# RWKV preparation moved into the loop of the mixing projection in a bidirectional encoder layer on one core

## The reference, cut to what matters

```python
proj = h @ w_in
gla_p, rw_p = proj[..., :GLA_COLS], proj[..., GLA_COLS:]
...
prev = jnp.pad(rw_p[:, :-1], ((0, 0), (1, 0), (0, 0)))
nxt = jnp.pad(rw_p[:, 1:], ((0, 0), (0, 1), (0, 0)))
rw = rw_p + rwkv_mu_prev * (prev - rw_p) + rwkv_mu_next * (nxt - rw_p)
r, kr, vr, wd_f, wd_b, ad, gd = _split(rw, RWKV_SPLITS)
...
dec_f = decay(wd_f, rwkv_w0_fwd, rwkv_w_up_fwd)
dec_b = decay(wd_b, rwkv_w0_bwd, rwkv_w_up_bwd)
a = jax.nn.sigmoid((rwkv_a0 + ad @ rwkv_a_up).astype(f32))
gate = (jax.nn.sigmoid(gd) @ rwkv_g_up).astype(f32)
kk = heads(kr * rwkv_k_k, RWKV_HEAD)
kk = kk / jnp.maximum(jnp.sqrt(jnp.sum(jnp.square(kk), axis=-1, keepdims=True)), 1e-12)
k2 = heads(kr * (1.0 + (a - 1.0) * rwkv_k_a), RWKV_HEAD)
```

## Time and profile before

| what | us |
|---|---|
| median of 3 runs | 4152.99 (4149.44 to 4160.55) |
| the profiled execution's own time | 4160.51 |
| its span, from first to last instruction | 4158.5 |
| mixing projection, first matmul to the store of the last tile | 1033.9 to 1417.2 |
| GLA | 1421.6 to 1656.6 |
| preparation, first load issued to first load of the recurrence | 1657.55 to 1839.88 |

### The profile page before, as it was taken

How to read it: one execution, slowest core, us unless ns; L and a number is a source line. 1 busy time by engine, 2 the same in 40 slices (tenths; PEclk the granted TensorE clock), 3 DMA queues, 4 the chain that set the end, 5 groups by cost and what they waited for, 6 DMA issues and landing times. The chain is left out here.

```text
span 4158.5 us, 68522 instructions
## 1 busy us (share of the span) xinstructions
PE 3614.8 (87%) x28536; PEld 3070.8 (74%) x28536; DVE 1872.7 (45%) x2671; ACT 927.5 (22%) x1295; POOL 225.8 (5%) x348
## 2 busy tenths in 40 slices
PE   7999999996999737449989688887897999999997
PEld 6888888885888536238888566776786888888885
DVE  4445444546000275765555532421225444444446
ACT  2111111103111245532323332222213111111112
POOL 0000000000000043012222100000000000000000
PEclk9999999998999868779999889998998999999999
DMA  2101010101222201652222122001001010101001
GB/s 107 46 30 45 30 45 30 45 5 42 109 79 87 114 1 42 195 183 91 75 74 75 73 98 109 15 31 41 31 26 41 31 45 30 45 30 45 30 20 51
DMA packets 70891, 243.80 MB, mean 59 GB/s; under 512 B 5056, under 2 KB 30912, under 8 KB 64448
## 3 DMA queue, kind: packets, MB, share of 16 engines
q1 hardware_dynamic: 64528, 219.39, 15.0%
q10 hardware_dynamic: 6192, 21.89, 1.3%
HBM read 185.22 MB, written 56.05 MB: 58 GB/s over the span
## 5 line engine op out<-in xcount | busy, mean ns | idle before, releaser
L292 DVE TENSOR_TENSOR main_acc<-main_acc,ffn_psum 128x512 f32<-128x512 f32 (+1 forms) x1056 | 617.7, 598 | 853.6 <-PE ffn_psum L215 853.0
L204 PE MATMUL ffn_psum<-x_xh,ffn_wi_h 128*128 128x512 f32 (+1 forms) x2112 | 525.1, 357 | 49.0 <-DVE ffn_wi_l L281 49.0
L204 PE MATMUL ffn_psum<-x_xh,ffn_wi_l 128*128 128x512 f32 (+1 forms) x2112 | 525.1, 357 | 0.0
L204 PE MATMUL ffn_psum<-x_xl,ffn_wi_h 128*128 128x512 f32 (+1 forms) x2112 | 525.0, 357 | 0.0
L204 PEld LDWEIGHTS ffn_psum<-x_xh,ffn_wi_h 128*128 128x128 f32 x2112 | 372.6, 188 | 116.9 <-DVE ffn_wi_l L281 49.4
L204 PEld LDWEIGHTS ffn_psum<-x_xh,ffn_wi_l 128*128 128x128 f32 x2112 | 349.8, 188 | 60.6
L204 PEld LDWEIGHTS ffn_psum<-x_xl,ffn_wi_h 128*128 128x128 f32 x2112 | 349.3, 188 | 61.1
L215 PE MATMUL ffn_psum<-ffn_hid_h,ffn_wo_h 128*128 128x512 f32 (+1 forms) x1056 | 380.5, 360 | 12.7 <-DVE ffn_hid_l L300 10.0
L215 PE MATMUL ffn_psum<-ffn_hid_h,ffn_wo_l 128*128 128x512 f32 (+1 forms) x1056 | 377.5, 358 | 0.0
L215 PE MATMUL ffn_psum<-ffn_hid_l,ffn_wo_h 128*128 128x512 f32 (+1 forms) x1056 | 376.6, 357 | 0.0
L256 ACT CAST ffn_hid_h<-ffn_hid 128x1280 fp32r<-128x1280 f32 x44 | 55.6, 1264 | 1090.4 <-DVE ffn_hid L298 1090.4
(11 more groups left out here) (303 smaller groups left out, 5629.2 us busy)
## 6 DMA issues: line engine op xcount, KB each, us to landing
ffn_w_raw_in<-ffn_w_in_dram SPq DMA_DIRECT2D x44, 1024.0 KB, 7.2
rws_pack<-pack SPq DMA_DIRECT2D x40, 900.0 KB, 6.3
ffn_w_raw_out<-ffn_w_out_dram SPq DMA_DIRECT2D x44, 512.0 KB, 3.5
proj<-mixin_stage ACTq DMA_DIRECT2D x27, 640.0 KB, 3.0
mixin_w_raw<-mix_w_in_dram SPq DMA_DIRECT2D x27, 512.0 KB, 3.4
pack<-rwp_pack SPq DMA_DIRECT2D x4, 2580.0 KB, 10.6
rwp_raw<-proj SPq DMA_DIRECT2D x15, 640.0 KB, 8.8
kv_w_raw<-ca_w_kv_dram SPq DMA_DIRECT2D x16, 512.0 KB, 3.5
```

The costliest lines, as they stand in the source:

```text
L204: mm = nc.tensor.matmul(ps[:, at + c * BANK:at + c * BANK + tn], w[:, slot, cols], x[:, k, t0:t0 + tn], start=(k == 0 and j == 0), stop=(k ...
L292: nc.vector.tensor_tensor(acc[:, o, t0:t0 + tn], acc[:, o, t0:t0 + tn], ps[:, at:at + tn], ALU.add).then_inc(added, 1)
```

## The change

The 27 tiles come in another order (by a new order of the weight columns): three low-rank tiles first, then for each group kr, r, vr, then the twelve GLA tiles. `linear_phase` for the mixing projection becomes `mixin_phase`, written out without a loop. The RWKV tiles are no longer stored to DRAM: ACT scales them straight out of PSUM and DVE adds the shifted copies from PSUM, each as one operation on 20 chunks of 63 columns and two on the chunk edges. The preparation's f32 matmuls (four products and two head sums per group, three chunks each) stand between k steps, one after a k step, into two further PSUM banks that are freed chunk by chunk; sigmoids, gate copies, clamps and bonus work on chunks. A PSUM set of an RWKV tile is free when its shifts are done (`next_added`). ACT and DVE run the steps of the preparation in a fixed order between the weight splits. The six work tiles lie in `main_acc`, once the residual has gone to DRAM (`spilled`). SP's queue holds weights, pack, gate and bonus stores in one order. The tile that holds the GLA gates' low-rank inputs is also stored raw. `rwkv_prepare_phase` and its loads are gone. `free_piece` waits until the piece two before (the same bank) was read; `high_part`, `low_part` and `project` are the old L386, L418 and one k step; `stayed` is L1075 with PSUM as its input, behind a wait for the tile's product; `logs` holds the old L1133 to L1146.

```diff
-Q_TILE, K_TILE, V_TILE, G_TILE = 0, 2, 4, 8
-R_TILE, KR_TILE, VR_TILE = 12, 16, 20
-DECAY_TILE, LOW_TILE, GATE_TILE = 24, 25, 26
-MIX_TILES = 27
+Q_TILE, K_TILE, V_TILE, G_TILE, LOW_TILE = 0, 2, 4, 8, 12
+GLA_TILES = 13
+N_LOW, N_RKV = 3, 12
+N_GLA = N_LOW + N_RKV
+MIX_TILES = N_GLA + 12
...
+        decay, aa, gate, run, kr, sums = [acc[:, 0], acc[:, 1]], acc[:, 2], acc[:, 3], acc[:, 4], acc[:, 5], acc[:, 6]
...
+            at = (6 + piece(kind, t, c) % 2) * BANK
+            return ps[:, at:at + TOKEN_CHUNKS[c][1]]
...
         @block.sync
         def _(sp):
...
+            weight(2)
+            weight(3)
...
+            sp.dma_start(resid_d, acc).then_inc(spilled, 16)
+            weight(4)
+            weight(5)
+            sp.wait_ge(low_copied, 1)
+            sp.dma_start(proj_d[LOW_TILE], low[:, 2]).then_inc(low_stored, 16)
+            weight(6)
             for t in range(4):
+                weight(tile(KR, t) + 4)
+                weight(tile(R, t) + 4)
                 sp.wait_ge(b_packed, t + 1)
                 sp.dma_start(pack_d[:, :, t, K_COL:PACK].rearrange("c p w -> p c w"), pack[:, :, K_COL:PACK]).then_inc(stored_b, 16)
+                sp.wait_ge(gate_done, NC * (t + 1))
+                sp.dma_start(gate_d[:, t], gate).then_inc(gate_stored, 16)
...
+                weight(tile(VR, t) + 4)
+                sp.wait_ge(centred, 4 * (t + 1))
+                sp.wait_ge(next_added, 3 * (tile(VR, t) + 1))
+                sp.dma_start(pack_d[:, :, t, 0:K_COL].rearrange("c p w -> p c w"), pack[:, :, 0:K_COL]).then_inc(stored_a, 16)
+                sp.wait_ge(bonus_done, NC * (t + 1))
+                sp.dma_start(bonus_d[:, t], sums).then_inc(bonus_stored, 16)
...
         @block.tensor
         def _(pe):
...
+            def logits(kind, t, c):
+                j, src, ready = {F_SIG: (0, 0, 1), B_SIG: (1, 0, 1), AA: (2, 1, 0), GATE: (3, 2, 2)}[kind]
...
+                free_piece(kind, t, c)
+                nc.tensor.matmul(piece_ps(kind, t, c), lora[:, t % 2, j * P:(j + 1) * P], low[:, src, tokens(c)],
+                                 start=True, stop=True).then_inc(pieced, 1)
+
+            def head_sums(kind, t, c):
+                pe.wait_ge(ones_in, 16)
+                pe.wait_ge((squared, rk_done)[kind == RK], t + 1)
+                free_piece(kind, t, c)
+                nc.tensor.matmul(piece_ps(kind, t, c), head_ones[:], sums[:, tokens(c)], start=True, stop=True).then_inc(pieced, 1)
...
+            def begin(n):
+                pe.wait_ge(split, n + 1)
+                if N_GLA <= n - 2:
+                    pe.wait_ge(emptied, n - 2 - N_GLA + 1)
+                elif n >= 2:
+                    pe.wait_ge(next_added, 3 * (n - 1))
...
             for t in range(4):
+                begin(tile(KR, t))
+                for k in range(KT):
+                    project(tile(KR, t), k)
+                    if t and 2 <= k < 5:
+                        head_sums(RK, t - 1, k - 2)
+                    if k >= 5:
+                        logits(AA, t, k - 5)
+                begin(tile(R, t))
+                for k in range(KT):
+                    project(tile(R, t), k)
+                    if k < 3:
+                        logits(F_SIG, t, k)
+                    if k >= 5:
+                        head_sums(KK, t, k - 5)
+                begin(tile(VR, t))
+                for k in range(KT):
+                    project(tile(VR, t), k)
+                    if k < 3:
+                        logits(B_SIG, t, k)
+                    if k >= 5:
+                        logits(GATE, t, k - 5)
+            for n in range(N_GLA, MIX_TILES):
...
         @block.scalar
         def _(act):
...
             for t in range(4):
                 if t:
+                    act.wait_ge(b_packed, t)
+                for c in range(NC):
+                    sigmoid(AA, t, aa, A0 + t, c)
...
+                stayed(tile(KR, t), view(kr), 4 + t)
+                high_part(tile(KR, t) + 2)
...
+                for c in range(NC):
+                    sigmoid(F_SIG, t, decay[0], W0 + t, c)
+                act.wait_ge(kk_raw, t + 1)
+                if t:
+                    act.wait_ge(bonus_stored, 16 * t)
+                nc.scalar.activation(view(sums), part(KK_COL), ACT.Square).then_inc(squared, 1)
+                if t:
+                    act.wait_ge(stored_a, 16 * t)
+                stayed(tile(R, t), part(R_COL), t)
+                high_part(tile(R, t) + 2)
+                for c in range(NC):
+                    sigmoid(B_SIG, t, decay[1], W0 + 4 + t, c)
+                act.wait_ge(clamped, NC * (t + 1))
...
+                stayed(tile(VR, t), part(V_COL), 8 + t)
+                high_part(tile(VR, t) + 2)
...
         @block.vector
         def _(dve):
...
+                nc.vector.scalar_tensor_tensor(dst[:, :, 1:], src[:, :, :-1], mu_p, dst[:, :, 1:], ALU.mult, ALU.add).then_inc(prev_added, 1)
+                for c0, cn in SEQ_CHUNKS:
+                    nc.vector.scalar_tensor_tensor(dst[:, c0 + 1:c0 + cn, 0:1], src[:, c0:c0 + cn - 1, C - 1:C], mu_p,
+                                                   dst[:, c0 + 1:c0 + cn, 0:1], ALU.mult, ALU.add).then_inc(prev_added, 1)
...
             for t in range(4):
+                shift(tile(KR, t), view(kr), 4 + t)
+                if t:
+                    dve.wait_ge(stored_b, 16 * t)
+                dve.wait_ge(next_added, 3 * (tile(KR, t) + 1))
+                nc.vector.tensor_scalar(part(KK_COL), view(kr), vecs[:, K_K + t:K_K + t + 1], None, ALU.mult).then_inc(kk_raw, 1)
+                low_part(tile(KR, t) + 2)
...
+                logs(t, 0)
+                for c in range(NC):
+                    dve.wait_ge(pieced, piece(KK, t, c) + 1)
...
+                shift(tile(R, t), part(R_COL), t)
+                low_part(tile(R, t) + 2)
...
+                logs(t, 1)
...
+                shift(tile(VR, t), part(V_COL), 8 + t)
+                low_part(tile(VR, t) + 2)
...
-        rwkv_prepare_phase(nc, a, proj_d, pack_d, vecs, side_d[0], side_d[1], consts)
...
-    proj_d = nc.dram_tensor("proj", (MIX_TILES, P, T), F32, kind="Internal").ap()
+    proj_d = nc.dram_tensor("proj", (GLA_TILES, P, T), F32, kind="Internal").ap()
...
-            linear_phase(nc, "mixin", weights, MIX_TILES, xh, xl, TOKEN_CHUNKS, "store", proj_d, spill=(acc[:], resid_d))
+            mixin_phase(nc, weights, a, xh, xl, acc[:], resid_d, proj_d, pack_d, vecs, side_d[0], side_d[1])
...
+    rkv = [u[:, t * P:(t + 1) * P] for t in range(4) for u in (kr, r, vr)]
+    out["mix_w_in"] = output_tiles(np.concatenate([wdf, wdb, ad, gdf, gdb, pad, gd] + rkv + [q, k, v, gg], 1))
```

More of the change, by code:

```diff
@@ L1060, in _ @@
+            for n in range(N_GLA, MIX_TILES):
+                begin(n)
+                for k in range(KT):
+                    project(n, k)
+                    if n == N_GLA and 2 <= k < 5:
+                        head_sums(RK, 3, k - 2)
         @block.scalar
         def _(act):
[L1062 to L1065 removed]
@@ new lines, in sigmoid @@
+            def sigmoid(kind, t, dst, bias, c):
+                act.wait_ge(pieced, piece(kind, t, c) + 1)
+                nc.scalar.activation(dst[:, tokens(c)], piece_ps(kind, t, c), ACT.Sigmoid, bias=vecs[:, bias:bias + 1]).then_inc(sig_done, 1)
+            high_part(0)
+            high_part(1)
+            stayed(0, view(low[:, 0]), 12)
+            high_part(2)
+            act.wait_ge(product, 2)
+            nc.scalar.copy(low[:, 2], slot(1)).then_inc(low_copied, 1)
+            act.wait_ge(low_copied, 1)
@@ L1097, in _ @@
-                nc.scalar.activation(raw[:, 1], raw[:, 1], ACT.Exp, scale=-0.5).then_inc(rooted, 1)
+                for c in range(NC):
+                    act.wait_ge(pieced, piece(GATE, t, c) + 1)
+                    nc.scalar.copy(gate[:, tokens(c)], piece_ps(GATE, t, c)).then_inc(gate_done, 1)
+                stayed(tile(VR, t), part(V_COL), 8 + t)
+                high_part(tile(VR, t) + 2)
+            for n in range(N_GLA, MIX_TILES):
+                i = n - N_GLA
+                act.wait_ge(product, n + 1)
+                if i >= 2:
+                    act.wait_ge(stored[n % 2], 16 * (i // 2))
+                nc.scalar.copy(stage(n), slot(n)).then_inc(emptied, 1)
+                act.wait_ge(emptied, i + 1)
+                act.dma_start(proj_d[i], stage(n)).then_inc(stored[n % 2], 16)
+                high_part(n + 2)
@@ L1099, in _ @@
+            for s in stored:
+                act.wait_ge(s, 16 * 6)
         @block.vector
@@ L1157, in _ @@
-                dve.wait_ge(kk_summed, t + 1)
-                nc.vector.tensor_scalar(raw[:, 1], sets[0], KK_EPS * KK_EPS, None, ALU.max).then_inc(clamped, 1)
+                nc.vector.tensor_tensor(part(K_COL), part(K_COL), view(kr), ALU.mult).then_inc(k_packed, 1)
+                logs(t, 0)
+                for c in range(NC):
+                    dve.wait_ge(pieced, piece(KK, t, c) + 1)
```

(9 more changed lines are left out.)

298 lines of the change are left out of this document (145 added, 153 removed).

## The result

The changed kernel takes 4023.0 us (median of 4 runs, 4018.0 to 4028.3), the kernel before, run beside it, 4151.2 us (4142.1 to 4160.6): a ratio of 0.969 with a 95% interval of [0.968, 0.971]. The profiled execution took 4018.0 us, with a span of 4015.9. Forecast were 4023.7 us, and 4031.2 for a profiled execution.

The account below looks back on a forecast made before the run. PE was taken to bound the projection, and a latency chain round the engines the preparation. -182.3 + 51.6 + 1.4 = -129.3 us against the median 4153.0 gave 4023.7 us; range for 8 in 10, 4012 to 4050.

Parts of the forecast that it names:

- Removed: Preparation, from SP's first load of it to the recurrence's first load: all of it goes, -182.3 us.
- Added on PE: Projection: 24 sets of 1280 f32 columns at 2.15 us each, at the projection's full clock, +51.6 us.
- sign of "about 437 us": New projection: if right, PE is busy above 98% of about 437 us, first matmul to last store.
- Joints 0: Projection: the 72 places where f32 matmuls stand between fp32r ones cost 0; high end 33 us.
- Waits of PE 0: Projection: PE never waits for ACT or DVE, cost 0; tightest at the key's square, slack 3 us.
- Rival 1: Projection: PE waits at some insertions for the square, bonus store or a bank; up to 33 us, chance 0.12.
- Block end: End of the projection's block: 30 more semaphores to clear, +1.4 us.
- fifth rival: Recurrence starts at a better moment of the clock: under 5 us faster than the sum, chance 0.03.
- Exposed loads: Projection: 144 weight loads of the insertions, 0.19 us each, don't overlap matmuls; 27 us, 4051 us, chance 0.04.
- preparation that doesn't fit: Projection: a blocked in-order queue makes the groups pace the stage; 74 us come back, 4098 us, chance 0.05.
- slower end: Twelve RWKV tiles: PE waits for the PSUM set and drops to half clock; 168 us, 4192 us, chance 0.02.

Follow-up runs that it names:

- e3: The changed kernel with each of the 72 inserted f32 matmuls issued twice into the same bank; 4074.2 us, ratio 0.981.
- e7: The changed kernel with the key's head sums three k steps earlier, after k steps 2, 3 and 4; 4034.7 us, ratio 0.972.
- e8: The changed kernel with a 5 MB store to DRAM ahead of each bonus store on SP's queue; 4046.9 us, ratio 0.975.
- e6: The changed kernel with a tile's matmuls waiting for DVE's shifts of the tile just before, as with one PSUM set; 4128.5 us, ratio 0.995.
- e5: The changed kernel with the three chunks of each inserted set together instead of one per k step; 4037.3 us, ratio 0.973.
- e9: The changed kernel with thirty more semaphores in the projection's block, used by nothing; 4024.6 us, ratio 0.971.
- e4: The changed kernel with head sums taking only the high half of their input, rounded to fp32r by an added ACT copy; 4021.5 us.
- e2: The kernel before with the loop over the mixing projection's 27 tiles written out and nothing else; 4167.5 us, ratio 1.003.
- e11: The kernel before with 128 waits, satisfied at once, on PE's queue behind its last GLA matmul; 4153.6 us, ratio 1.001.

## Why the prediction was right

**Removed, -182.3: right.** The stretch from GLA's first load to the load of `pack` lost 183.4 us; what is left behind GLA is a gap of 0.94 us, as long as the one that stood there before the preparation. The 1.1 us beyond the forecast are GLA itself, whose stretch varies by 2 us among the runs.

**Added on PE, +51.6: right.** Measured +51.3, and the same sets once more cost 52.3 (e3). Taking the price at the clock of the stage to which the work moves, and not the 78 us that it cost at the old one, was the choice that carried the sum. The prediction's sign of "about 437 us" for the stage is not what its terms give (383.3 + 51.6 = 434.9); 434.5 were measured.

**Joints 0: right.** PE has no idle time behind the first weights, and 0.84 to 0.86 us per 512 columns were read. The 351 us of weight loads lie under 433 us of matmuls in 434.5, and an insertion's price goes by its columns and not by its two loads (e3). The Trainium skill (TensorE: Matmul & The Clock Gate, Part 3, What overlaps and what doesn't) has a load overlap matmuls only in another row group; these are loads of all 128 rows, and the trace doesn't agree.

**Waits of PE 0: right, and on the estimated margin.** The square was forecast to end at T + 10 and to be wanted at T + 13.1. Tile kr of group 1 ends at T = 1149.1, where its last insertion starts; the square ended at 1158.8, T + 9.7, and was wanted at 1162.2, T + 13.1. The bonus store was forecast to land at T + 6 and landed at T + 5.8. DVE was put at about 35 us of a group and has 34.1, ACT at 22 and has 21.4, a shift at 1.49 and is 1.53. e7, e8 and e6 take away this cover in three ways, and each turns into idle PE at once; e5 does so for the PSUM banks. Rival 1 was thus a matter of 3 us of slack, and the slack held.

**Block end +1.4: right in kind, low in size.** 30 semaphores more cost 1.7 us in the change, and 2.2 us when added alone (e9).

**What the sum lacks.** The stages up to the load of `pack` give +51.3 + 1.7 - 183.4 + 0.3 = -130.1 and the medians differ by 128.2, against a forecast of 129.3. The two profiled executions differ by 142.5, since the one of the kernel before lies 9.3 us over its median and the one of the changed kernel 5.0 under its own. 12.1 us of that lie in the recurrence and its end, whose instructions the change doesn't touch. Its first 24 us and the 36 behind them, before and after:

```profile
1839.88:1863.88 24.00, 15.67 (x327) 14.73 (x329) 13.76 (x23) 6.69 (x18) 10.80 (x18) 0.72 0.61 232
1863.88:1899.88 36.00, 32.30 (x981) 30.95 (x979) 19.45 (x46) 11.48 (x32) 5.56 (x10) 1.00 0.29 106
```

```profile
1709.82:1733.82 24.00, 15.94 (x369) 15.00 (x371) 14.94 (x26) 7.24 (x20) 10.79 (x18) 0.77 0.60 233
1733.82:1769.82 36.00, 32.47 (x897) 31.06 (x894) 17.39 (x41) 11.01 (x31) 5.56 (x10) 0.91 0.29 106
```

After the change the clock is higher at first (0.77 for 0.72) and 42 more matmuls fit into 24 us. This is no accident of one execution: in the same 24 us all three kernels with the old code have 0.72 to 0.73 and 313 to 327 matmuls, and all the others 0.76 to 0.78 and 340 to 373. But it doesn't last. In the next 36 us the clock is 0.91 against 1.00, and at 60 us the changed kernel is 42 matmuls behind (1266 against 1308). So the fifth rival's better moment of the clock is seen, and it doesn't explain the 12 us, which come about later. In the profiled executions the stretch takes 680 to 687 us in all three kernels with the old code and 667 to 675 in all the others but e4 (684.2). The medians have no room for 12 us of it. Why profiled executions show it isn't settled.

The mechanism and its terms are borne out stage by stage. That the forecast of 4023.7 came within 0.7 us of the median is luck: single runs spread over 10 us, 12 us of difference in the recurrence have no cause, and neither has e2's 14 us. The changed kernel is written out too, and whether it carries such a cost isn't known.

**The rivals.** Exposed loads (4051 us) fall by the stage's 51.3 us and e3's 52.3, and the preparation that doesn't fit (4098) by the groups of 55.1 us. The slower end needed 10.8 us in each of twelve tiles. e6 forces a stop in each of 14 tiles, and it costs 7.6 us per tile (106.6 / 14), 5.4 idle and the rest at the lower clock. The mechanism is real, and stays below its break-even.

## What to carry to other kernels

A stage bound by a chain round several engines can be laid between the steps of a stage bound by one: it then costs only what that engine must do for it, at that stage's clock, which here was 51 us for a stage of 182. It needs each result to be asked for later than its chain delivers it, so work out the tightest due time in rows before writing the order, since a few us of slack were all there was. A stop of the bounding engine is to be priced at more than its idle time, as the lower clock behind it added two fifths here.

## What the runs showed of the hardware

- A stop of 5.4 us in an otherwise gapless stream of matmuls cost 7.6 us in all (75.3 us idle, 31.3 us more of busy time over 14 recorded stops), as the granted clock fell behind it. The 6.9 us stops of e8 cost 9.5. The 1.8 us stops of e7 left the granted clock at 1.00.
- An f32 product between fp32r matmuls costs 2.14 us per 1280 columns where it stands singly (51.3 / 24) and 2.18 for each further one behind an equal one (e3); 0.84 us per 512 columns and 0.42 per 256 were read.
- Thirty semaphores that nothing uses made the end of their block 2.2 us longer, 0.07 us each (e9, one trace).
- The recurrence began at a higher granted clock in all eleven traces without the preparation before it than in the three with it (0.76 to 0.78 against 0.72 to 0.73 over 24 us), and the lead was gone after 60 us in the pair looked at.
- Writing out one loop, with no change in its own stage (382.2 for 382.0 us), made the kernel 14 us slower elsewhere (e2), while 128 more waits on PE's queue left it 4.9 us above the kernel before, with an interval from 0 to 9 (e11). The cause of the 14 us is open.
